# Last down weights with their first input half first, and the output stored in four half-row transfers

## The reference, cut to what matters

```
h = rms_norm(x, norm_ffn)
for e in range(32):
    hid = silu(h @ w_gate[e]) * (h @ w_up[e])           # 256 hidden inputs
    y = y + combine[..., e:e + 1] * (hid @ w_down[e])   # w_down[e]: 256 x 1024
x = x + y
return x * rsqrt(mean(x * x) + 1e-6) * norm_final
```

## Time and profile before

| | |
|---|---|
| median of 3 runs | 639.82 us (639.82 to 640.83) |
| the profiled execution: its own time | 641.12 us |
| the profiled execution: span | 639.3 us |
| PE busy | 600.1 us (94%) |
| DVE busy, ACT busy | 216.1 us (34%), 144.6 us (23%) |
| mean DMA rate, bytes read from HBM | 247 GB/s, 157.07 MB |

### The profile page before, as it was taken

One profiled execution on the slowest core, in us unless ns is written; L12 is line 12 of the kernel. 1 busy time (PEld: TensorE's weight loads), 2 busy tenths in 40 slices (PEclk: granted clock), 3 DMA queues, 4 the chain that ended last, 5 costly groups with the idle time before them and its releaser, 6 DMA issues.

```text
span 639.3 us, 11809 instructions
## 1 busy us (share of the span) xinstructions
PE 600.1 (94%) x4968; PEld 433.5 (68%) x4968; DVE 216.1 (34%) x586; ACT 144.6 (23%) x366; POOL 19.9 (3%) x23
## 2 busy tenths in 40 slices
PE   7999999999999999999999999998989888977794
PEld 7988887878877777778888888884435424524331
DVE  3152348616344676456211322233110111011022
ACT  3110234042234453444330000001201110110023
POOL 1000000000300103001000000000000000000000
PEclk9999999999999999999999999997999989979798
DMA  8584344741211222112336997978999999999993
GB/s 313 201 330 164 125 145 166 311 145 67 80 55 69 68 68 68 68 29 107 121 99 254 422 420 280 424 316 312 421 421 419 420 420 421 421 420 420 422 390 124
DMA packets 27415, 158.95 MB, mean 249 GB/s; under 512 B 3024, under 2 KB 7264, under 8 KB 9568
## 3 DMA queue, kind: packets, MB, share of 16 engines
q1 hardware_dynamic: 24352, 137.71, 55.2%
q10 hardware_dynamic: 3008, 20.45, 7.7%
HBM read 157.07 MB, written 1.07 MB: 247 GB/s over the span
## 4 chain that ended last, share of the span: by engine, by line
PE 59%; issue 22%; DMA 8%; SPq 5%; DVE 4%; ACT 1%; POOL 0%; POOLq 0%; DVEq 0%; ACTq 0%
PE bank L620 25%; PE bank L1235 7%; DMA ring<-experts 6%; PE bank L1299 4%; SPq L583 4%; PE bank L1244 4%; PE bank L846 3%; PE bank L1308 3%; PE bank L652 2%; PE bank L955 2%; PE bank L984 2%; DMA ring<-front 1%; PE bank L1004 1%; DVE work L1810 1%; PE bank L968 1%
## 5 line engine op out<-in xcount | busy, mean ns | idle before, releaser
L620 PE MATMUL bank<-hT,ring 128*128 128x256 f32 x864 | 199.6, 383 | 0.5 <-ACTq L1447 0.3
L620 PEld LDWEIGHTS bank<-hT,ring 128*128 128x128 f32 x864 | 159.6, 190 | 30.7 <-issue 10.6
L620 PE MATMUL bank<-yT,ring 128*128 128x256 f32 x256 | 55.4, 379 | 0.0
L620 PEld LDWEIGHTS bank<-yT,ring 128*128 128x128 f32 x256 | 48.6, 190 | 6.6
L1299 PE MATMUL bank<-ring,work 128*32 128x512 f32 (+1 forms) x192 | 37.8, 697 | 7.8 <-DMA yT<-experts 6.5
L1810 DVE TENSOR_TENSOR work<-bank,table 128x512 f32<-128x512 f32 (+1 forms) x22 | 11.6, 544 | 94.5 <-PE bank L1244 88.8
L1244 PEld LDWEIGHTS bank<-work,tok 128*128 128x128 f32 x256 | 31.4, 198 | 11.1 <-issue 11.1
L1435 ACT ACTIVATE work<-bank 128x512 f32<-128x512 f32 (+2 forms) x45 | 23.3, 518 | 51.9 <-PE bank L1299 40.8
L1244 PE MATMUL bank<-work,tok 128*128 128x128 f32 x256 | 33.0, 285 | 0.5 <-DVEq L2319 0.5
L1308 PE MATMUL bank<-work 128*128 128x512 f32 (+1 forms) x68 | 30.4, 584 | 1.3 <-ACT work L1435 0.7
L1235 PE MATMUL bank<-ring,work 128*32 128x512 f32 x240 | 30.8, 623 | 0.1
(11 more groups left out here) (258 smaller groups left out, 721.0 us busy)
## 6 DMA issues: line engine op xcount, KB each, us to landing
ring<-front SPq DMA_DIRECT2D x47, 1024.0 KB, 5.1
ring<-experts SPq DMA_DIRECT2D x40, 1024.0 KB, 21.4
work<-experts SPq DMA_DIRECT2D x9, 1024.0 KB, 27.3
ring<-experts ACTq DMA_DIRECT2D x8, 1024.0 KB, 15.1
table<-experts SPq DMA_DIRECT2D x6, 1024.0 KB, 24.3
yT<-experts SPq DMA_DIRECT2D x6, 1024.0 KB, 26.4
hT<-experts SPq DMA_DIRECT2D x4, 1024.0 KB, 22.8
work<-experts ACTq DMA_DIRECT2D x3, 1024.0 KB, 28.0
```

What stands on the lines that cost most here:

```text
L620: return first(pe.matmul(o, l, r, start=(k == 0), stop=(k == n - 1)))
```

## The change

The last down weights are cut otherwise: piece 0 is input half 0 of all 1024 columns, then comes input half 1 in column groups of 512, 256 and 256. PE multiplies input half 0 of all three column groups as soon as piece 0 is there, and input half 1 group by group as pieces 1 to 3 come; the scatters keep their order, and those of group 1 now stand ahead of the wait for the last piece. The output is stored in four transfers of half rows (256 KB each): three by SP, one by ACT, which no longer waits for `final_ready`.

```diff
-PIECES = ((0, 1, 0, 512), (1, 2, 0, 512), (0, 2, 512, 256), (0, 1, 768, 256), (1, 2, 768, 256))
+PIECES = ((0, 1, 0, 1024), (1, 2, 0, 512), (1, 2, 512, 256), (1, 2, 768, 256))
...
             sp.wait_ge(q["final_ready"], 1)
+            sp.dma_start(out[0:P, 512:D], res[:, 0, 512:D]).then_inc(q["stored"], 16)
             sp.wait_ge(q["front_scaled"], 1)
-            sp.dma_start(out[0:P, :], res[:, 0, :]).then_inc(q["stored"], 16)
-            sp.wait_ge(q["stored"], 16 * NT)
+            sp.dma_start(out[0:P, 0:512], res[:, 0, 0:512]).then_inc(q["stored"], 16)
+            sp.wait_ge(q["final_ready"], NT)
+            sp.dma_start(out[P:S, 512:D], res[:, 1, 512:D]).then_inc(q["stored"], 16)
+            sp.wait_ge(q["stored"], 16 * 2 * NT)
...
-                        down_part(bank[0], *LAST[0], fs=(0,))
+                        for n in range(len(LAST)):
+                            down_part(bank[(0, 1, 4)[n]], *LAST[n], fs=(0,))
                         pe.wait_ge(q["late_loaded1"], 16 * GANG)
                         down_part(bank[0], *LAST[0], fs=(1,))
                         scatter_last(0, 0)
                         pe.wait_ge(q["late_loaded2"], 16 * GANG)
-                        down_part(bank[1], *LAST[1])
+                        down_part(bank[1], *LAST[1], fs=(1,))
                         scatter_last(0, 1)
-                        pe.wait_ge(q["late_loaded3"], 16 * GANG)
-                        down_part(bank[4], *LAST[2], fs=(0,))
                         scatter_last(1, 0)
                         scatter_last(1, 1)
-                        pe.wait_ge(q["late_loaded4"], 16 * GANG)
+                        pe.wait_ge(q["late_loaded3"], 16 * GANG)
                         down_part(bank[4], *LAST[2], fs=(1,))
                         scatter_last(2, 0)
                         scatter_last(2, 1)
...
                 act.wait_ge(q["front_scaled"], NT)
-                act.wait_ge(q["final_ready"], NT)
-                act.dma_start(out[(NT - 1) * P:NT * P, :], res[:, NT - 1, :]).then_inc(q["stored"], 16)
+                act.dma_start(out[P:S, 0:512], res[:, 1, 0:512]).then_inc(q["stored"], 16)
```

More of the change, by code:

```diff
@@ L366, in build_layer @@
             "moe_ready", "member_ready", "crowd_ready", "sel_ready", "wsel_ready", "dense_chain", "gath_ready",
-            "ghid_ready", "final_ready", "hT2_ready", "gains_ready", "gains_spread", "gfin_ready", "late_loaded1", "late_loaded2", "late_loaded3", "late_loaded4", "squared", "last_total", "last_in", "last_root", "front_gained", "front_scaled", "dve_chain"]
+            "ghid_ready", "final_ready", "hT2_ready", "gains_ready", "gains_spread", "gfin_ready", "late_loaded1", "late_loaded2", "late_loaded3", "squared", "last_total", "last_in", "last_root", "front_gained", "front_scaled", "dve_chain"]
         q = {n: sem(n) for n in names}
```

## The result

The changed kernel took 641.2 us (median of 20 runs, 640.12 to 642.99), the kernel before 640.06 us in the runs beside it (20 runs, 639.17 to 641.17). The ratio is 1.0015, with a 95% interval of 1.0008 to 1.0022: about 1.0 us slower (0.5 to 1.4; the two medians are 1.1 us apart), less than the 0.2% that a measurement can be sure of. The forecast was +1.4 us.

The account below looks back on a forecast made before the run. The end hangs on finishing column group 0 and the PE, ACT and DVE work after it; +1.55 us for later last scatters less 0.15 for the stores gives +1.4, 641.2 us, range 639.9 to 642.3 (8 in 10).

Parts of the forecast that it names:

- the forecast case: Whole kernel: the change makes it +1.0 to +2.0 us slower (640.8 to 641.8), chance 0.58.
- the landing is not what holds group 0: Last down weights: piece 1 lands well ahead of 624.6 and stalls overlap better; +0.3 to +1.0 us, chance 0.14.
- What sets the end: End of kernel: it hangs on when column group 0 can be finished (622.22 us before) and the engines' work after.
- The landing: Last down weights: piece 0 lands at 621.85 us; piece 1 at 624.6, making group 0's input half 1 2.4 us later.
- rival of +2.25: Last transfers: row length gains nothing or the stores cost more, piece 1 at 625.2, total 642.1 us; chance 0.12.
- What the moved matmuls give, and the stall: PE behind piece 1: moving input half 0 of groups 1 and 2 saves 1.07 us; a new DVE stall costs 0.35.
- The clock at the end: PE's new pauses before piece 0, before piece 1 and under ACT's copy: the granted clock holds, no cost.
- The stores: Output stores: the first starts 0.34 us sooner, shorter rows lose 0.11; between 0.34 gain and 0.1 loss.
- the term of 0.15 us: Output stores: the gain taken for the four half-row stores, 0.15 us.
- The straggler: Last output bytes: rival that the lagging transfer engine ends with the others, 639.4 us, not slower; chance 0.12.

Follow-up runs that it names:

- e7: Kernel before with the four half-row stores, piece 0 widened to 768 columns and only group 1's input half 0 moved ahead of piece 1; -0.2 us against before.
- e6: Kernel before with the four half-row stores, piece 2 split by input half, group 1's half 0 multiplied during ACT's copy; -0.6 us against before.
- e4: Changed kernel with piece 0 loaded as two pieces of 2 KB rows instead of one of 4 KB rows; +1.9 us against the kernel before.
- e3: Changed kernel with DVE copying each column group before it multiplies a gain; +0.7 us against the kernel before.
- e2: Kernel before with only the four half-row stores, pieces and PE's order as before; -1.1 us by the ratio, median 639.69 against 640.32.
- e10: Kernel before with five filler matmuls instead of two in PE's routing-stage pause, nothing else; ratio 0.9998 against before.
- e9: e6 with five filler matmuls instead of two in PE's routing-stage pause; 638.64 us, ratio 0.9984 against the kernel before.
- e5: e3 with PE multiplying group 1's input half 1 ahead of the first scatter and DVE's copies on their own semaphore; +0.4 us against before.

## Why the prediction was right, point by point

The mechanism is the forecast's, but the time says it less clearly than the legs. The measured 641.2 is the very figure of the forecast, and that is luck: the kernel before took 0.24 us more in these runs than the 639.82 of the forecast, and the change cost 1.0 to 1.1 us instead of 1.4. The forecast gave 0.53 to a kernel slower by over 1.3 us and 0.42 to one within 0.2%, and the less likely of the two came. The +1.0 also lies where the forecast case ends and the rival "the landing is not what holds group 0" begins (+0.3 to +1.0). It is the landing of piece 1 and leg 1 that decide for the forecast.

- **What sets the end.** Right: the landing of piece 1 and the work behind it. e7 and e6 show both sides of it.
- **The landing.** Right. Piece 1 was put at 624.6 - 616.79 = 7.8 us behind the chunk; it came at 7.84. Piece 0 was put at 5.06 and landed at 5.1. PE began on it only at 5.44, with no effect, as PE was idle for 0.47 us ahead of piece 1 even so. By e4 the longer rows bring about 0.3 us of the 0.37 that the forecast gave them (622.22 less 621.85), if it isn't the smaller number of transfers. The rule of the Trainium skill (DMA: Bandwidth & Descriptors, Specifications), line rate from 512 B on, would have had e4 and the change land together; the trace disagrees by these 0.28 us at piece 1. The forecast isn't quite of one piece there: it gives +2.0 us by that rule, and then puts it with a rival of +2.25.
- **What the moved matmuls give, and the stall.** Right: 24 instructions in 1.93 us (forecast 2.1), DVE's stall 0.34 us (0.35), leg 1 14.90 us (630.04 - 615.14), where the forecast's steps give 631.68 - 616.79 = 14.89. The price of the stall itself was 0.51 us by e3, as the wait also lays weight loads bare.
- **The clock at the end.** Right: PE's pauses there cost nothing in leg 1. What I didn't see is that the profile of before held a fall of the clock at 436 us which the runs' median need not hold. I only noted that the profiled execution lay 1.3 us above the median. The fall changed no leg, as both are counted from the chunk.
- **The stores.** The start was right: the first issue comes 0.36 us sooner (0.34 forecast). Whether the term of 0.15 us was too small is open. Leg 2 shrank by 0.5 in the pair of profiles, but scatters by 0.3 inside each kind of store, and by more with e10. In timed runs the stores alone gave 1.1 us by the ratio (0.4 to 1.8), 0.6 by the medians, and 0.35 among the executions at a mean clock of 0.978 or more; the first lies outside the bounds (0.34 gain to 0.1 loss), the last at their edge. In the profiles leg 1 rose by 1.60 where the forecast had 1.55, so the step from +1.4 down to +1.0 lies in leg 2, by the stores or by its scatter.
- **The straggler.** I gave 0.12 to a rival in which the last transfer engine ends with the others. Neither e2 nor the change shows it. e10's leg of 8.3 us (8.9 and 9.2 in the others with full rows) and e9's of 8.1 (8.65 to 9.0 with half rows) show that the end can come 0.5 us or more sooner with the same stores, whether by the code ahead or by the chip. That instruction fetches are the cause was argued from the queues' shares only, and isn't shown.

Open: how much the four stores are worth, what places the trickle, and whether the fall of the clock in the routing stage is what makes the chunk late.

## What to carry to other kernels

Work moved ahead of a transfer is worth only what it puts into a real pause; count what the transfer behind it now delays, and which copies and stalls had been hidden under the old wait. If a load is cut in pieces, put first what the longest chain behind it needs, as before and e6 do, not what lets the most matmuls run. When two profiles are compared, anchor both at an event ahead of the change: here an upstream shift of 1.65 us made a loss of 1.1 us over both legs look like a gain of 0.6 in the span.

## What the runs showed of the hardware that was not expected

- The granted clock in the routing stage, behind a stretch in which PE was busy for 0.61 to 0.71 of 2 us, fell in four of ten profiles (before, e2, e4, e5) and not in the other six, with the same code in that stage. Where it fell, the last gate and up chunk landed 1.3 to 2.7 us later (616.8 to 617.6 against 614.9 to 615.5). That one is the cause of the other fits in size but wasn't tested.
- The last output bytes are moved by little more than one transfer engine for the last 1 to 2 us (27 to 30 GB/s, a share of 0.06 to 0.09 before). How long that goes on isn't fixed: ten slices of 0.15 us with the change, six with e10, by other code or another chip.
- Three small scatters in a row cost 0.5 us less than the same three with one 0.34 us wait among them (1.92 against 2.46 us, e3 and the change).
